# Order of the first products of a one-core transformer kernel: the norm weights' turn, the bias table and the zeroed products

## What is computed

```python
# first_block, layer 0
hn   = rms_norm(x, norm_mix_g[0])              # x * rsqrt(mean(x^2) + eps) * g
proj = hn @ w_in                               # q, k, v, and u for the pooling
bias_dist = rel_bias[t5_bucket(arange(S))].T   # (4 heads, 256 distances)
o = diff_attention(q1, q2, k1, k2, v, lam, bias_dist)   # logits + bias_dist[q - k], causal
y = multi_scale_pool(u, pool_w, pool_scale)
h = x + concat([o, y]) @ w_out
# then cross attention and an MLP, a second layer with a gated convolution,
# and second_block: forgetting attention, retention and an MLP
```

## Time and profile before

| | |
|---|---|
| median of 3 runs | 1092.77 us (1092.53 to 1093.17) |
| the profiled execution's own time | 1092.15 us |
| its span, first to last instruction | 1090.3 us |
| TensorE busy | 1081.8 us, 99% of the span |
| VectorE, ScalarE, GpSimd busy | 726.7, 524.6, 60.2 us |
| DMA | 225.16 MB, mean 206 GB/s |

### The profile page before, as it was taken

One profiled execution on the slowest core, in us unless ns is written; L12 is line 12 of the kernel. 1 busy time (PEld: TensorE's weight loads), 2 busy tenths in 40 slices (PEclk: granted clock), 3 DMA queues, 4 the chain that ended last, 5 costly groups with the idle time before them and its releaser, 6 DMA issues.

```text
span 1090.3 us, 14099 instructions
## 1 busy us (share of the span) xinstructions
PE 1081.8 (99%) x5877; PEld 932.5 (86%) x5877; DVE 726.7 (67%) x790; ACT 524.6 (48%) x601; POOL 60.2 (6%) x109
## 2 busy tenths in 40 slices
PE   8999999999999999999999999999999999999998
PEld 7998898898888888998888888888888887888886
DVE  5666566477777677766646877769767488574654
ACT  6655455354534445344545353544565465453441
POOL 2200000000000000000001000000201010000000
PEclk9999999999999999999999999999999999999999
DMA  9844553466785746554645768575334463655531
GB/s 343 333 175 174 193 197 132 174 213 249 267 336 209 298 164 217 186 190 156 218 151 206 284 257 336 210 297 181 119 145 165 151 254 120 225 193 193 193 116 39
DMA packets 33071, 225.16 MB, mean 206 GB/s; under 512 B 4288, under 2 KB 4484, under 8 KB 8560
## 3 DMA queue, kind: packets, MB, share of 16 engines
q1 hardware_dynamic: 26784, 187.97, 46.9%
q0 software_dynamic: 5824, 35.64, 9.3%
q10 hardware_dynamic: 400, 0.64, 0.2%
HBM read 223.16 MB, written 1.87 MB: 206 GB/s over the span
## 4 chain that ended last, share of the span: by engine, by line
PE 97%; DVE 1%; DMA 1%; ACT 1%; issue 0%; POOL 0%; ACTq 0%
PE ps L540 48%; PE ps L521 19%; PE ps L497 11%; PE ps L524 10%; PE ps L853 1%; PE ps L832 1%; PE ps L701 1%; PE ps L601 1%; DMA work<-in_rel_bias 1%; PE ps L996 0%; PE ps L1042 0%; DVE lo L1713 0%; PE ps L611 0%; PE ps L1054 0%; PE ps L975 0%; PE ps L842 0%
## 5 line engine op out<-in xcount | busy, mean ns | idle before, releaser
L1713 DVE TENSOR_TENSOR lo<-raw,hi 128x2048 fp32r<-128x2048 f32 x160 | 365.9, 2289 | 173.6 <-ACT hi L1185 173.2
L1185 ACT ACTIVATE hi<-raw 128x2048 fp32r<-128x2048 f32 x160 | 306.0, 1914 | 257.9 <-PE ps L540 142.1
L521 PE MATMUL ps<-xt,hi 128*128 128x512 f32 x896 | 245.4, 395 | 0.0
L540 PE MATMUL ps<-hi,yt_hi 128*128 128x512 f32 x544 | 213.5, 392 | 0.0
L540 PE MATMUL ps<-hi,yt_lo 128*128 128x512 f32 x544 | 212.0, 390 | 0.0
L540 PE MATMUL ps<-lo,yt_hi 128*128 128x512 f32 x544 | 211.9, 390 | 0.0
L521 PEld LDWEIGHTS ps<-xt,hi 128*128 128x128 f32 x896 | 154.3, 189 | 21.5
L524 PEld LDWEIGHTS ps<-xt,lo 128*128 128x128 f32 x896 | 137.3, 189 | 19.0
L524 PE MATMUL ps<-xt,lo 128*128 128x256 f32 x896 | 142.4, 281 | 0.0
L540 PEld LDWEIGHTS ps<-hi,yt_lo 128*128 128x128 f32 x544 | 102.1, 188 | 21.5
L540 PEld LDWEIGHTS ps<-hi,yt_hi 128*128 128x128 f32 x544 | 102.2, 188 | 20.6
(11 more groups left out here) (282 smaller groups left out, 1095.6 us busy)
## 6 DMA issues: line engine op xcount, KB each, us to landing
raw<-in_weights SPq DMA_DIRECT2D x174, 1024.0 KB, 4.9
work<-in_w_ada POOLq DMA_DIRECT2D x16, 1536.0 KB, 7.6
work<-in_gains POOLq DMA_DIRECT2D x6, 512.0 KB, 4.2
work<-mod_rows POOLq DMA_DIRECT2D x6, 512.0 KB, 6.1
raw<-in_weights SPq DMA_DIRECT2D x4, 512.0 KB, 7.6
h<-in_x SPq DMA_DIRECT2D x2, 512.0 KB, 4.2
work<-in_mem POOLq DMA_DIRECT2D x2, 512.0 KB, 8.0
work<-in_pool SPq DMA_DIRECT2D x1, 1024.0 KB, 12.1
```

Of the source, the lines that this page charges most:

```text
L521: pe.matmul(o, hi[:, slot, k, js], flat(x[2][:, b * HC + k]), start=(b == 0 and k == 0), stop=False, skip_group_check=True)
L540: mm = pe.matmul(ps[:, n, :], xs[:, c, t * P:(t + 1) * P], ws[:, slot, k, :], start=(first and k == 0 and i == 0), stop=(last and k == HC ...
L1185: act.activation(hi[:, p % RING], raw[:, p % RING], ACT.Copy).then_inc(hi_ready, 1)
L1713: dve.tensor_tensor(lo[:, p % RING], raw[:, p % RING], hi[:, p % RING].bitcast(F32), ALU.subtract)\
```

## The change

Four moves, all ahead of or just behind the first unit; nothing of the result changes.

- TensorE makes nine zeroed products ahead of the transpositions instead of five, and six behind them instead of three.
- The turn of the norm weights moves from before `first_rows(0)` to between `first_rows(0)` and `first_rows(1)`.
- The bias product moves from between the two `first_rows` to behind `first_unit`, and from bank 3 to bank 6.
- ACT's copy of it moves from behind the first of eight chunks to behind the eighth, ahead of `hi_half(2)`.

```diff
         def bias_rows():
             pe.wait_ge(loaded["rel"], 32)
-            o = claim(3, "bias_row")
+            o = claim(6, "bias_row")
...
         pe.wait_ge(zeroed, 1)
-        zero_products(5)
+        zero_products(9)
         pe.wait_ge(loaded["ident"], 16)
+        first_rows(0)
         pe.wait_ge(loaded["gain_mix0"], 16)
         o = claim(3, "gain_col")
         filled_by(pe.transpose(o[:, 0:KC], gain_rows, ident[0:KC, 0:KC]), "gain_col")
-        first_rows(0)
+        first_rows(1)
+        zero_products(6)
+        first_unit(UNIT["l0_u"])
         bias_rows()
-        first_rows(1)
-        zero_products(3)
-        first_unit(UNIT["l0_u"])
         unit_w(UNIT["l0_q"], XT, (2, 3))
...
         first_hi(0)
         for c in range(KC):
             hi_chunk(c // HC, c % HC)
-            if c == 0:
-                act.wait_ge(*fill("bias_row"))
-                act.activation(bias_row[0:4, :], bank("bias_row")[0:4, 0:384], ACT.Copy).then_inc(*free("bias_row"))
             if c % 2 and c + 1 < KC:
                 first_hi((c + 1) // 2)
+        act.wait_ge(*fill("bias_row"))
+        act.activation(bias_row[0:4, :], bank("bias_row")[0:4, 0:384], ACT.Copy).then_inc(*free("bias_row"))
         for k in range(2, RING):
             hi_half(k)
```

## The result

The changed kernel takes 1096.56 us (median of 6 runs, 1095.96 to 1097.15) against 1092.65 us (6 runs, 1092.41 to 1093.17) for the kernel before: a ratio of 1.0036 with a 95% interval of 1.0026 to 1.0047. It is slower, by 3.9 us.

A forecast was written before the change was run, and what follows sets the result against it. TensorE was taken to bound the kernel, through its clock and a three-engine chain at the start. 1092.15 - 2.8 (early start) + 5.6 (row behind the first unit) = 1094.95, plus half the median's difference: 1095.2 us; range 1094.2 to 1097.6.

The forecast's parts named there:

- the rivals of the clock: Clock falls in the pause before `l0_q` (0.25, 1095.9 to 1097.6), or rises late before the first unit (0.05, 1096.5).
- the fall in the pause: Clock drops during the 4.9 us pause, so `l0_q` starts at the lower level: +3.7 to +5.5 us; chance 0.25.
- What bounds the kernel: TensorE, busy 99%; its settling into the stream depends on the clock and an ACT-DVE-TensorE chain of 2.41 us.
- The start of the first unit: First real product at 9.8 instead of 12.63, 2.8 us earlier; ACT starts at about 7.4, the chain adds 2.41.
- end (a) of the three: Lowest bound on the first unit's start: weights land at 8.03, ACT's and DVE's chunks add 0.6 and 0.7, giving 9.4.
- The row behind the first unit: Bias product, ACT's copy, ACT's and DVE's parts of half 2 in sequence: 5.6 us until `l0_q`, 4.9 a new pause.
- What is queued further back: Later work still arrives in time: half 4 with 2.5 us to spare, the bias masks with 1.2.
- the clock stays: Forecast's own case at the pause before `l0_q`: no fall of the clock, +2.4 to +3.2 us, 0.50.
- a sign of being wrong: At the start of `l0_q`: first products 0.24 apart instead of 0.12 would show a fallen clock.
- the term for the fallen clock: Lower-clock cost at `l0_q`: absent from the main sum, priced only in a rival at 1.2 to 2.9 us, chance 0.25.
- a rival at 0.05: Before the first unit, transpositions don't raise the clock: start at 11.4, +4.4 us, 1096.5; chance 0.05.
- Not slower: Rival at the first unit's start: 9.4 pays nearly all back, 1094.55 us, within 0.2% of before; chance 0.17.

The follow-up runs named there:

- e1: The changed kernel with ACT's copy of the bias product moved behind the two halves of `l0_q`; 1095.21 us.
- e2: The changed kernel with 20 zeroed products added behind the bias product, inside the pause; 1094.76 us.
- e9: The changed kernel with the bias product ahead of the first unit (bank 3), ACT's copy still behind the eighth chunk; 1089.80 us.
- e8: e1 with POOL's loads of the columns, lambda vectors and `mem` let out at the fourth rounded bank, ahead of the bias rows' store; 1090.28 us.
- e5: The kernel before with only the zeroed products' counts changed, to nine ahead and six behind; 1092.37 us.
- e4: e9 with ACT's copy of the bias product back behind the first chunk; 1090.13 us.
- e6: The changed kernel with the turn of the norm weights back ahead of the first rows; 1096.37 us.
- e10: e9 with three instead of six zeroed products behind the rows; 1089.44 us.
- e11: e9 with five zeroed products ahead and three behind, as in the kernel before; 1089.82 us.
- e3: The changed kernel with five zeroed products ahead and three behind, as in the kernel before; 1097.71 us.

## Why the prediction was right, and what it missed

The direction, the place and most of the mechanism came out as forecast: a wait in ACT's queue costs TensorE more than the early start gives. The forecast itself was 1095.2 us (1094.6 to 1095.6), though, and the measured 1096.56 lies above it. It is inside the stated range because that also covered the rivals of the clock, and one of them, the fall in the pause, is what happened.

- **What bounds the kernel.** Right. The 4.0 us of the span are all in TensorE's first 30 us; its later waits are the same to 0.1 us.
- **The start of the first unit.** Forecast 9.8 with 9.4 to 10.3, measured 9.63. That the two are so close is in part luck. ACT's first copy at 6.88 came even before the 7.4 of the sum, since the clock was up at about 5.2 and not at 6.5 to 7; what then bound was the landing of the first weights at 1.64 + 6.56 = 8.20, end (a) of the three. When the clock comes up differs between executions with the same start: the first eight transpositions took 1.04 to 1.92 us in the eight profiled executions that begin with nine zeroed products and show them in a row of their own.
- **The row behind the first unit.** Forecast 5.6 us, measured 5.55; the pause 4.9, measured 4.7; the start of `l0_q` 26.45, measured 26.23. Each link is in the chain above, close to the duration taken from before.
- **What is queued further back.** Forecast: it holds. It did. Half 4 was split at 34.4, where the sum had 35.5, and TensorE came for it at about 39.2; the bias masks were done at 60.7, where the sum had 66.1, and DVE came for them at 68.4. The masks were early because the copy of the rows took 20.2 us instead of 24.7. Why it did is not shown: the DMA engines' mean share over the copy was 0.90 in both kernels. The slack that I gave half 4 was thin, though: in e1, where TensorE began `l0_q` 4.5 us earlier, it was short by 3.1.
- **The clock in the pause.** Here the forecast missed. I took "the clock stays" as likeliest (0.50) and its fall as a rival with 0.25. It fell: in the profile 4.2 us into the pause, with the first products of `l0_q` 0.22 apart instead of 0.12, which I had named as a sign of being wrong; and in each of the six runs the mean granted clock is 0.997 or 0.998. The step that failed is the term for the fallen clock, put at nothing in the sum; it measured 1.5 us in the chain and at most 1.8 by e2. It rested on the last row of rows 4: TensorE idle for 3.8 us at the end of the span with the clock still up. I let it stand for a pause of 4.9 us, although the pause was longer than the row, and the row is one execution. The same last stretch shows how little one execution tells: the clock fell within it in five of the twelve profiled executions (last section). The rival's price, +3.7 to +5.5 us, 1095.9 to 1097.6, holds the measured time, but its upper bound was loose: at most 4.6 us at the lower level cost 2.3, not the 2.9 that it used. The rule of the Trainium skill, "TensorE: Matmul & The Clock Gate", section "Why this matters for your kernels", is that an idle gap between bursts of matmuls costs the clock. The prediction set it aside because no row of before showed such a fall; the pauses of 4.7 us here and 3.1 us in e1 agree with the rule.
- **The other rule of the Trainium skill**, that transpositions do not bring the full clock ("TensorE: Matmul & The Clock Gate", section "Part 4: PE-mode transpose"), made a rival at 0.05. These runs do not bear it out: the clock stayed up through 16 transpositions in a row (5.18 to 7.27) in the changed kernel, and e9 shows it rising among the first eight, with nine zeroed products ahead of them.
- **Not slower.** Did not happen: the early start gave 3.0 us against 7.05.
- **Where the slower time comes from** was named before: ACT's queue. e9 shows it from one side, and e1 together with e8 from the other.

## What to carry to other kernels

When an operation moves later on one engine, look at the engines that wait for it: everything behind that wait in their queues moves with it, DMAs included, and the fix of one queue can uncover the next (e1, then e8). A small product that nobody needs soon belongs where its producer is waiting anyway, here in the 0.9 us before the first unit, not behind it. And price a new pause of TensorE at more than its length: here 4.7 us cost 6.2 to 6.5.

## What the runs showed of the hardware

TensorE's clock falls more readily than I had taken it to. It fell in or just after pauses of 4.7 us (the changed kernel), 3.1 us (e1) and 2.0 us (e5, 1.8 us into it), while it stayed up through 1.5 us in e8.

The end of the span is the best comparison, since TensorE is idle there for the last 3.9 us in every kernel, behind the same work. This is the changed kernel's window on it (busy time by engine, then PEclk, DMA share, GB/s):

```profile
1090.40:1094.30 3.90, 0.00 (x0) 0.00 (x0) 1.38 (x2) 0.00 (x0) 0.00 (x0) 0.97 0.25 92
```

In the kernel before and in e2, e4, e6, e8, e9 and e10 the granted clock of the last 3.9 us is 1.00. In five others it is lower: 0.97 here, 0.88 in e11, 0.82 in e1, 0.77 in e3 and 0.76 in e5, where it fell 3.7, 2.9, 2.5, 2.1 and 2.0 us after TensorE's last product. So idle stretches of the same length behind the same work end differently from one execution to the next, and one row with the clock still up does not show that a pause is safe. The stretch at the lower level differed too: after the same pause of 4.7 us it ran to 29.0 in the changed kernel and to 32.8 in e3. I can't say from these runs what decides.
